# RWKV systems solved in three batches with both directions on 128 partitions, scan offset 4 instead of 8, delta rows padded to 16 bytes

## The chip, the cores and the metric

The kernel runs on one core of a Trainium2 chip. The metric is the device time of one execution in microseconds, as the median of several executions. An execution can be profiled; its profile lists every instruction of the engines PE (TensorE), DVE (VectorE), ACT (ScalarE), POOL (GpSimd) and the DMA issues of SP, ACT and POOL.

## What is computed

Two blocks run one behind the other: a gated convolution with differential attention, and a block whose mixer is half gated delta rule (8 heads of 128) and half RWKV-7 (16 heads of 64), each in both directions over 256 context and 512 latent positions. The change is in the mixers of the second block.

```python
CHUNK = 64
def gated_delta_chunked(q, k, v, beta, g, s0):
    ...
    tmat = lax.linalg.triangular_solve(eye + lmat, eye, left_side=True, lower=True, unit_diagonal=True)
    u = tmat @ (v * beta[..., None])
    wk = tmat @ (kb * jnp.exp(g)[..., None])
    ...
def rwkv7_scan(r, w, k, v, kk, b_vec, s0):
    def step(state, inp):
        sa = -jnp.einsum('bhvk,bhk->bhv', state, kk_t)
        state = (state * w_t[:, :, None, :] + sa[..., None] * b_t[:, :, None, :]
                 + v_t[..., None] * k_t[:, :, None, :])
        return state, jnp.einsum('bhvk,bhk->bhv', state, r_t)
    ...
```

The reference steps RWKV position by position. The kernel does it, like the delta rule, in chunks of 64 positions (12 chunks per direction, the first four of them context, whose outputs aren't needed), and each chunk of each head and direction needs the inverse of a unit triangular 64x64 matrix, called a system here.

## The kernel before

**The systems.** They are formed by the two preparation stages and lie in the tensor `systems`, as 64x64 images, (2 directions) x (96 of the delta rule + 192 of RWKV). `Solver` holds one batch of 96 systems of one direction, one per partition. GpSimd solves it in place (`substitute`): the two 32x32 blocks on the diagonal are inverted in 31 steps of two TENSOR_TENSOR instructions each, L2637 and L2639; `turn` then writes ones on the diagonal (L2645) and two transposed copies (L2652, L2653), from which the scan later builds the off-diagonal block. Direction 2's systems are eliminated backwards (the argument `d`). `begin` fetches a batch (L2665), `end` stores it (L2674), both from GpSimd's own queue. There are six batches: delta, and two of RWKV, for each direction.

**`rwkv_prep`** works through eight pairs of heads, `i`. PE, DVE and ACT form the operands and the systems of pair `i` in direction `d`; SP stores them (`RwkvPrep.store`, L2997 to L3013, the systems at L3000) and counts them in `stored`. Beside that GpSimd solves the batches (0, 0), (0, 1), (1, 0) whole and (1, 1) for `SPLIT` = 20 steps; (1, 0) waits for the stores of the first four pairs.

**`scans`** runs the delta rule's chunks (`DeltaScan`, g) and RWKV's (`RwkvScan`, r) in one loop over n. Loop n holds delta step n and RWKV step n - `LAG`, with `LAG` = 8, so there are 20 loops: eight with a delta step alone, four with both, eight with an RWKV step alone. The order of each engine is written out by hand in one block per engine. GpSimd finishes batch (1, 1), then solves (2, 0) in a room that is later an operand buffer, and (2, 1) in its first room; after that it only zeroes quarters of loaded inverses (`clear`, L3580). SP loads operands two steps ahead: `DeltaOperands.load` has four transfers a step (channel rows L3161 of 129 columns and token rows L3162 of 321), `load_inverse` two (L3167), `RwkvScan.load` eight or twelve, `RwkvScan.load_inverse` four (L3432). In loop `LAG` - 2 SP waits until all stores of GpSimd have landed and loads the first three steps' RWKV inverses. `RwkvScan.middle` (L3444) is the first PE work on an inverse; it stands in the PE's order in loop n for step n + 1 - `LAG`, so everything behind it waits with it. The outputs of the delta steps from 4 on are formed in a bank of their own (`go`) and stored by ACT (`store`). From loop 12 on the PE also folds one head's outputs per loop (`out.fold`), eight in all.

**`closing`** multiplies by the last weights and normalises; it isn't changed.

## Time and profile before

| | us |
|---|---|
| median of 3 runs | 3967.39 (3965.67 to 3968.11) |
| the profiled execution | 3961.41 |
| its span | 3959.7 |
| granted PE clock in it, share of full | 0.932 |
| busy: PE, PEld, DVE, ACT, POOL | 3479.2, 2771.7, 2075.4, 665.0, 787.4 |
| RWKV preparation | 2823 to 3207 |
| scan loops | 3207 to 3694 |
| head outputs, closing | 3694 to 3960 |

All times of the trace are microseconds from the start of the span. PEld is the PE's loading of weights, which overlaps its matmuls. "POOL L2639 TENSOR_TENSOR" is GpSimd's instruction of line 2639. Names such as `all_sn`, `scan_rops` are tiles: `all_sn` is the solver's room, `scan_rops` the RWKV operands (and the second solver's room), `scan_rinv` the RWKV inverses, `all_gchan` and `all_gtok` the delta operands. "SPq" is SP's DMA queue. An instruction's idle time before it stands in brackets with what released it.

### The profile page before, as it was taken

To read this page: it belongs to the slowest core of one execution; us is meant where nothing else is said; L and a number is where in the kernel's file an instruction comes from. 1 tells how busy PE (TensorE), PEld (TensorE's weight loads), DVE (VectorE), ACT (ScalarE), POOL (GpSimd) and SP (SyncE) were. 2 spreads that over 40 slices of the span, in tenths; PEclk is the share of its full clock that TensorE was granted. 3 is DMA by queue.
4 is the path that set the end of the run, shared out by engine and by line. 5 is a ranking of instruction groups with operands and counts; after the bars stand their busy time and mean duration, and the time that the engine had idled before them with its cause. 6 is when DMAs were issued, how large, how long until landed. Compare 5 with 4: busy or idle time off the path is not lost. (4 is left out here: it accounts for less than half of the span.)

```text
span 3959.7 us, 64096 instructions
## 1 busy us (share of the span) xinstructions
PE 3479.2 (88%) x28192; PEld 2771.7 (70%) x28192; DVE 2075.4 (52%) x2261; ACT 665.0 (17%) x1079; POOL 787.4 (20%) x817
## 2 busy tenths in 40 slices
PE   6999999999998989889999999999677725677698
PEld 3777777777787878778888888876466625576386
DVE  2477777753333545544463353329678725332564
ACT  2122222212000001210110010002234301221100
POOL 0111111111000000025005216100375799000000
PEclk8999999999999999999999999999689867888799
DMA  9444444444333453322232223337578798777243
GB/s 400 145 152 147 157 155 149 151 175 161 116 118 111 164 188 138 112 90 88 84 113 86 89 101 107 115 112 258 187 186 225 190 228 169 173 228 213 74 175 106
DMA packets 359079, 607.73 MB, mean 153 GB/s; under 512 B 136441, under 2 KB 244081, under 8 KB 330129
## 3 DMA queue, kind: packets, MB, share of 16 engines
q1 hardware_dynamic: 305488, 472.23, 37.8%
q0 software_dynamic: 21712, 92.42, 7.1%
q10 hardware_dynamic: 31600, 38.99, 2.8%
q8 instruction: 222, 3.64, 0.4%
q14 instruction: 57, 0.46, 0.0%
HBM read 469.17 MB, written 134.39 MB: 152 GB/s over the span
## 5 line engine op out<-in xcount | busy, mean ns | idle before, releaser
L182 PE MATMUL front_ps<-b_hT,p_wb 128*128 128x512 f32 x4224 | 979.3, 392 | 6.8 <-PEq L94 6.8
L182 PEld LDWEIGHTS front_ps<-b_hT,p_wb 128*128 128x128 f32 x4224 | 789.9, 188 | 187.3 <-issue 20.6
L1772 PE MATMUL in_ps<-b_hT,in_wb 128*128 128x512 f32 (+1 forms) x3264 | 750.7, 391 | 13.3 <-DVE in_wb L1759 13.3
L1772 PEld LDWEIGHTS in_ps<-b_hT,in_wb 128*128 128x128 f32 (+1 forms) x3264 | 607.1, 187 | 148.1 <-DVE in_wb L1759 13.5
L1757 DVE CAST in_wb<-in_raw 128x2048 fp32r<-128x2048 f32 (+1 forms) x68 | 82.6, 1215 | 536.4 <-PE in_ps L1772 531.5
L170 DVE CAST p_wb<-p_raw 128x2048 fp32r<-128x2048 f32 x88 | 108.0, 1227 | 430.4 <-PE front_ps L182 419.1
L813 POOL DMA_DIRECT2D front_mwb<-in_w_ada x128 | 101.3, 796 | 794.4 <-PE front_mps L823 788.8
L1772 PEld LDWEIGHTS in_ps<-b_hc,in_wb 128*128 128x128 f32 (+1 forms) x1728 | 211.4, 189 | 3.2
L1772 PE MATMUL in_ps<-b_hc,in_wb 128*128 128x256 f32 (+1 forms) x1728 | 212.6, 283 | 0.0
L172 DVE TENSOR_TENSOR p_wb<-p_raw,p_wb 128x2048 fp32r<-128x2048 f32 x88 | 201.8, 2293 | 3.0
L1211 PE MATMUL mid_ps<-mid_wb,b_hT 128*128 128x512 f32 x768 | 178.2, 393 | 14.0 <-DVE mid_wb L1196 14.0
L1081 PE MATMUL merge_ps<-b_hT,merge_wb 128*128 128x512 f32 x768 | 178.5, 395 | 12.5 <-DVE merge_wb L1069 10.1
L480 DVE SCALAR_TENSOR_TENSOR bf_both<-front_up,front_taps,bf_both 128x512 f32<-128x512 f32 x240 | 180.4, 752 | 11.8
L1211 PE MATMUL last_ps<-last_wb,last_pair 128*128 128x512 f32 x768 | 175.9, 392 | 11.3 <-DVE last_wb L1196 11.3
L1081 PEld LDWEIGHTS merge_ps<-b_hT,merge_wb 128*128 128x128 f32 x768 | 146.1, 191 | 44.9 <-DVE merge_wb L1069 10.5
L1211 PEld LDWEIGHTS mid_ps<-mid_wb,b_hT 128*128 128x128 f32 x768 | 144.5, 189 | 44.1 <-issue 14.4
L1211 PEld LDWEIGHTS last_ps<-last_wb,last_pair 128*128 128x128 f32 x768 | 145.2, 189 | 43.1 <-issue 12.8
L2639 POOL TENSOR_TENSOR all_sn<-all_sn 96x62 f32<-96x62 f32 (+15 forms) x155 | 173.0, 1116 | 12.2
L1759 DVE TENSOR_TENSOR in_wb<-in_raw,in_wb 128x2048 fp32r<-128x2048 f32 (+1 forms) x68 | 173.9, 2557 | 2.3
L2007 POOL TENSOR_TENSOR in_mdx<-in_mx 128x255 f32<-128x255 f32 (+9 forms) x53 | 59.1, 1115 | 526.7 <-ACT in_mx L1984 524.5
L2637 POOL TENSOR_TENSOR all_sn<-all_sn 96x62 f32<-96x62 f32 (+15 forms) x155 | 154.1, 994 | 13.8 <-POOLq L94 1.7
L1790 POOL MEMSET in_gper_row<- 128x2 f32 x1 | 0.1, 99 | 679.4 <-POOLq L94 679.4
(452 smaller groups left out, 4289.0 us busy)
## 6 DMA issues: line engine op xcount, KB each, us to landing
p_raw<-in_w_in_tiles SPq DMA_DIRECT2D x88, 1024.0 KB, 6.1
in_raw<-in_w_in_tiles SPq DMA_DIRECT2D x67, 1024.0 KB, 4.8
front_mwb<-in_w_ada POOLq DMA_DIRECT2D x128, 512.0 KB, 5.0
open_wb<-in_w_ada_groups SPq DMA_DIRECT2D x32, 1024.0 KB, 11.3
g_scr<-gprep_ob SPq DMA_DIRECT2D x8, 3474.0 KB, 11.5
merge_raw<-in_w_branch_units SPq DMA_DIRECT2D x32, 512.0 KB, 4.6
mid_raw<-in_w_o_parts SPq DMA_DIRECT2D x32, 512.0 KB, 3.7
last_raw<-in_w_out_parts SPq DMA_DIRECT2D x32, 512.0 KB, 3.7
```

The source lines that it names most:

```text
L170: nc.vector.tensor_copy(self.wb[:, n % 2, 0], self.raw[:, n % 2]).then_inc(self.high_ok, 1)
L172: nc.vector.tensor_tensor(self.wb[:, n % 2, 1], self.raw[:, n % 2], self.wb[:, n % 2, 0].bitcast(F32), ALU.subtract).then_inc(self.w_split, 1)
L182: last = self.nc.tensor.matmul(self.ps[:, n % 2, :], self.wb[:, n % 2, x, kt, :], self.hT[:, y, kt, :], start=kt == term == 0, stop=kt == ...
L480: link(nc.vector.scalar_tensor_tensor(acc, u[:, j:j + T], self.taps[:, i, j:j + 1], acc, ALU.mult, ALU.add))
L813: pool.dma_start(self.wb[:, m % 2], w[m % 4, :, :, c:c + self.COLS]).then_inc(self.w_in[m % 2], 16)
L1081: last = self.nc.tensor.matmul(self.ps[:, u, :], self.wb[:, u, x, kt, :], self.pair[:, y, j, kt, :], start=kt == n == 0, stop=kt == self.C ...
L1211: last = self.nc.tensor.matmul(self.bank(i), self.pair[:, x, q * self.KQ + kt, t * P:(t + 1) * P], self.wb[:, n % 2, y, kt, :], start=q == ...
L1757: nc.vector.tensor_copy(high, raw).then_inc(self.high_ok, 1)
L1759: nc.vector.tensor_tensor(low, raw, high.bitcast(F32), ALU.subtract).then_inc(self.w_split, 1)
L1772: last = self.nc.tensor.matmul(self.ps[0:width, n % 3, first:end], self.wb[:, n % 2, x, kt, 0:width], h[:, y, kt, :], start=kt == term == ...
L2637: link(ops.tensor_tensor(t, y[:, :, a, j:j + 1].to_broadcast([BATCH, 2, na, ni]), y[:, :, j:j + 1, after].to_broadcast([BATCH, 2, na, ni]) ...
L2639: link(ops.tensor_tensor(y[:, :, a, after], y[:, :, a, after], t, ALU.subtract))
```

## The change

- **Systems.** RWKV's systems get a tensor of their own, `r_systems`, with images of 64 rows by `W` = 96 columns, of which 64 are filled at first and the other 32 later hold the transposed copy. Direction 2's systems are formed transposed (`turned_products`: 48 matmuls of 64 columns in place of 24 of 128 per pair), so that both directions are eliminated forwards, with 64 systems of each direction on 128 partitions: `fetch`, `eliminate`, `deliver`. RWKV then has three batches in place of four, each of 128 systems in place of 96. A batch is fetched in two transfers of 4,096 rows of 256 B (before, one of 96 rows of 16 KB) and stored in two of 64 rows of 24 KB. Batches 0 and 1 need 3 and 6 stored pairs (`ready_by`).
- **Where they run.** In the preparation: delta 0 and 1, RWKV batch 0, and 20 steps of batch 1. In the scan stage: the rest of batch 1, and batch 2, which SP fetches at the stage's start. The second solve in the first room, with its reload by SP, is gone.
- **`LAG`** = 4: 16 loops, four with a delta step alone, eight with both, four with RWKV alone, in which two heads are folded per loop. The inverses are waited for in loop 2.
- **Outputs of the delta steps** are formed in the work banks behind RWKV's `value_outputs`, and ACT stores them ahead of `r.complete`; RWKV has both output banks to itself.
- **Delta rows** are padded: channel rows from 129 to 132 columns (516 to 528 B), token rows from 321 to 324 (1,284 to 1,296 B).
- RWKV inverses are loaded with rows of 384 B in place of 256 B. Addresses move with the sizes, `sw` lies in `ex`, and `r.start` waits for the preparation's stores.

```diff
-G_CH, G_TOK = 2 * C + 1, C + 2 * GD + 1
+G_PAD = 4
+G_CH, G_TOK = 2 * C + G_PAD, C + 2 * GD + G_PAD
...
+W = C + HC
...
+def fetch(eng, m, r_systems, batch):
+    for d in range(2):
+        r = slice(HALF * d, HALF * (d + 1))
+        full = m.image[r].rearrange("p (i j) -> p i j", j=W)
+        eng.dma_start(full[:, :, HC:W], images_of(r_systems, batch, d).rearrange("p (i j) -> p i j", j=W)[:, :, HC:W]).then_inc(m.n_in, 16)
...
+def eliminate(ops, link, m, steps):
+    full, y = m.image.rearrange("p (i j) -> p i j", j=W), m.blocks
+    if steps.start == 0:
+        link(ops.memset(m.diagonal, 2.0))
+    for j in steps:
+        na, ni = j + 1, HC - 1 - j
+        a, after = slice(0, na), slice(na, HC)
+        t = full[:, HC:HC + na, 0:C].rearrange("p a (b y) -> p b a y", b=2)[:, :, :, 0:ni]
+        link(ops.tensor_tensor(t, y[:, :, a, j:j + 1].to_broadcast([P, 2, na, ni]),
+                               y[:, :, j:j + 1, after].to_broadcast([P, 2, na, ni]), ALU.mult))
+        link(ops.tensor_tensor(y[:, :, a, after], y[:, :, a, after], t, ALU.subtract))
...
+def deliver(pool, ops, link, m, r_systems, batch):
...
+    link(ops.memset(m.diagonal, 1.0))
+    flip = lambda x: x.rearrange("p i j -> p j i")
+    link(ops.tensor_copy(full[:, lo, first], flip(full[:, lo, middle])))
+    link(ops.tensor_copy(full[:, hi, first], flip(full[:, lo, last])))
+    link(ops.tensor_copy(full[:, hi, middle], flip(full[:, hi, last])))
+    pool.sem_inc(m.tick, 1)
+    for d in range(2):
+        pool.dma_start(images_of(r_systems, batch, d), m.image[HALF * d:HALF * (d + 1)]).then_inc(m.y_out, 16)
...
-                for n, (batch, d) in enumerate(((0, 0), (0, 1), (1, 0), (1, 1))):
...
+                for d in range(2):
...
+                    solve(nc, pool, link, solver, systems, d, d)
+                for batch in range(BATCHES - 1):
+                    for u in range(3):
+                        pool.wait_ge(m.stored[u], m.STORED * len(range(u, 2 * ready_by(batch), 3)))
+                    pool.wait_ge(solver.y_out, 32 * (batch + 1))
+                    pool.sem_inc(solver.tick, 1)
+                    fetch(pool, solver, r_systems, batch)
...
-LAG = 8
+LAG = 4
+FOLDS = GH // LAG
...
-                sp.dma_start(second.rows, rows_of(systems, 2, 0)).then_inc(second.n_in, 16)
+                fetch(sp, second, r_systems, BATCHES - 1)
                 before.finish_small(sp)
                 r.load(sp, 0)
-                sp.wait_ge(first.y_out, 64)
-                sp.dma_start(first.rows, rows_of(systems, 2, 1)).then_inc(first.again, 16)
...
                     if n == LAG - 2:
-                        sp.wait_ge(second.y_out, 16)
-                        sp.wait_ge(first.y_out, 80)
+                        sp.wait_ge(first.y_out, 32 * BATCHES)
+                        sp.wait_ge(second.y_out, 32)
```

How the instructions move, at two places. Names are tiles and tensors as above, and a row lists the semaphores that it waits for. First GpSimd in the preparation, where one batch is handed over to the next; before, from the first RWKV hand-over (end of the second delta batch, fetch of (1, 0)):

```order
L2652 COPY all_sn<-all_sn 96x32x32 [waits all_schain]
L2653 COPY all_sn<-all_sn 96x32x32 [waits all_schain]
L2674 DMA systems<-all_sn 96x4096 [waits all_schain]
L2665 DMA all_sn<-systems 96x4096 [waits all_sy_out,all_r_stored2,all_r_stored0,all_r_stored1]
L2630 MEMSET all_sn 96x64 [waits all_sn_in]
L2637 TENSOR_TENSOR all_sn<-all_sn 96x62 [waits all_schain]
L2639 TENSOR_TENSOR all_sn<-all_sn 96x2x31 [waits all_schain]
```

Now, at the hand-over from RWKV batch 0 to batch 1:

```order
L2721 MEMSET all_sn 128x64 [waits all_schain]
L2723 COPY all_sn<-all_sn 128x32x32 [waits all_schain]
L2724 COPY all_sn<-all_sn 128x32x32 [waits all_schain]
L2725 COPY all_sn<-all_sn 128x32x32 [waits all_schain]
L2728 DMA r_systems<-all_sn 64x6144 [waits all_schain]
L2728 DMA r_systems<-all_sn 64x6144
L2697 DMA all_sn<-r_systems 64x64x64 [waits all_sy_out,all_r_stored2,all_r_stored0,all_r_stored1]
L2697 DMA all_sn<-r_systems 64x64x64
L2705 MEMSET all_sn 128x64 [waits all_sn_in]
L2711 TENSOR_TENSOR all_sn<-all_sn 128x2x31 [waits all_schain]
```

A third copy stands ahead of the store, store and fetch are two transfers each, and the fetch has rows of 64 elements.

Second SP's queue at the start of the scan stage, behind the operands of RWKV step 0; before:

```order
L3410 DMA scan_rval<-v_scr 128x512
L3412 DMA scan_rval<-v_scr 64x512 [waits open_x_in0]
L3413 DMA scan_rval<-v_scr 64x512
L3823 DMA all_sn<-systems 96x4096 [waits all_sy_out]
L3161 DMA all_gchan<-g_scr 128x8x129 [waits p1_w_in0]
L3162 DMA all_gtok<-g_scr 64x8x321
L3161 DMA all_gchan<-g_scr 128x8x129
L3162 DMA all_gtok<-g_scr 64x8x321
```

Now:

```order
L3484 DMA scan_rval<-v_scr 128x512 [waits open_w_in4]
L3485 DMA scan_rval<-v_scr 128x512
L3487 DMA scan_rval<-v_scr 64x512 [waits open_x_in0]
L3488 DMA scan_rval<-v_scr 64x512
L3242 DMA all_gchan<-g_scr 128x8x132 [waits p1_w_in0]
L3243 DMA all_gtok<-g_scr 64x8x324
L3242 DMA all_gchan<-g_scr 128x8x132
L3243 DMA all_gtok<-g_scr 64x8x324
```

The reload of the first solver's room, with its wait for GpSimd's store, no longer stands ahead of the loads of delta step 2. Further down, the twelve loads of the first RWKV inverses stand ahead of the loads of delta step 5, where before they stood behind those of step 8.

## Rows read from the trace of the kernel before

**Rows 1.** Stretches: length; busy (count) of PE, PEld, DVE, ACT, POOL; clock; DMA share; GB/s.
```profile
2823.00:3207.00 384.00, 260.34 (x3632) 207.38 (x3632) 265.02 (x222) 126.31 (x137) 271.94 (x246) 0.80 0.74 184
3293.00:3348.00 55.00, 41.56 (x725) 36.36 (x723) 33.76 (x44) 11.60 (x24) 50.45 (x53) 0.87 0.92 189
3393.00:3425.00 32.00, 25.63 (x792) 22.91 (x783) 15.19 (x23) 6.94 (x15) 1.21 (x4) 0.89 0.57 110
3425.00:3487.00 62.00, 47.26 (x1375) 42.59 (x1370) 25.60 (x38) 13.93 (x31) 2.43 (x8) 0.81 0.79 197
3487.00:3511.00 24.00, 20.02 (x702) 18.34 (x690) 12.94 (x18) 5.98 (x12) 1.22 (x4) 0.93 0.76 229
3511.00:3694.00 183.00, 131.22 (x4896) 117.46 (x4883) 40.51 (x53) 29.71 (x64) 8.50 (x28) 0.86 0.71 212
```

**Rows 2.** PE waits, 3207 to 3380 us: line and releaser; total, times, longest.
```profile
PE scan_gpx L3444 <- DMA scan_rinv<-systems: 30.8, 1, 30.8
```

**Rows 3.** GpSimd in time, preparation: start, length, instruction, idle before and releaser.
```profile
2832.60 0.21 POOL L2630 MEMSET all_sn<- 96x64 f32 x1 [8.90 <-DMA all_sn<-systems]
...
2909.71 0.21 POOL L2645 MEMSET all_sn<- 96x64 f32 x1 [0.16 <-POOL all_sn L2639]
...
3016.76 0.53 POOL L2674 DMA_DIRECT2D systems<-all_sn  x1 [0.58 <-POOL all_sn L2653]
...
3047.94 0.54 POOL L2665 DMA_DIRECT2D all_sn<-systems  x1 [30.65 <-DMA systems<-rprep_ob]
...
3165.91 0.21 POOL L2630 MEMSET all_sn<- 96x64 f32 x1 [11.95 <-DMA all_sn<-systems]
...
3204.20 1.19 POOL L2639 TENSOR_TENSOR all_sn<-all_sn 96x480 f32<-96x480 f32 x1
```

**Rows 4.** Issues of the RWKV systems' stores, SP: count, ns min/median/max, first and last start.
```profile
L3000 SPq DMA_DIRECT2D systems<-rprep_ob x32: 574/655/1563, 2883.4 to 3194.9; - x32
```

**Rows 5.** GpSimd in time, scan stage.
```profile
3207.06 1.02 POOL L2637 TENSOR_TENSOR all_sn<-all_sn 96x462 f32<-96x462 f32 x1 [1.67 <-POOLq L94]
...
3226.85 0.21 POOL L2645 MEMSET all_sn<- 96x64 f32 x1 [0.15 <-POOL all_sn L2639]
...
3231.58 0.53 POOL L2674 DMA_DIRECT2D systems<-all_sn  x1 [0.59 <-POOL all_sn L2653]
...
3294.66 0.21 POOL L2645 MEMSET scan_rops<- 96x64 f32 x1 [0.15 <-POOL scan_rops L2639]
```

**Rows 6.** SP in time: last stores of the preparation, first inverse loads.
```profile
3201.74 3.64 SPq L3013 DMA_DIRECT2D r_mix<-rprep_ob  x2
...
3374.03 8.47 SPq L3432 DMA_DIRECT2D scan_rinv<-systems  x12
```

**Rows 7.** PE waits, 3393 to 3690 us, the first of the list.
```profile
PE scan_rwork L3462 <- issue: 26.9, 15, 3.9
```

**Rows 8.** Transfers issued from 3207 to 3690 us: count, size, median us to landing.
```profile
all_gtok<-g_scr SPq DMA_DIRECT2D x22, 642.0 KB, 11.9
scan_rops<-r_home SPq DMA_DIRECT2D x24, 528.0 KB, 5.2
...
all_gchan<-g_scr SPq DMA_DIRECT2D x22, 516.0 KB, 9.6
...
systems<-all_sn POOLq DMA_DIRECT2D x2, 1536.0 KB, 8.6
```

**Rows 9.** Transfers, 3376 to 3384 us: packets and the queue's share.
```profile
q1 hardware_dynamic: 5857, 1.47, 82.9%
```

**Rows 10.** GpSimd's transfers of 128 pieces (L2036) and of 512 (L813).
```profile
L2036 POOL DMA_DIRECT2D p<-in_mx x27: 593/602/1584, 1743.6 to 2493.8; - x27
...
DMA to landing us min/median/max: 2.3/2.7/4.3
L813 POOL DMA_DIRECT2D front_mwb<-in_w_ada x128: 748/748/1563, 118.8 to 1010.1; - x128
...
DMA to landing us min/median/max: 4.0/5.0/8.6
```

More of the change, by code:

```diff
@@ L2607, with substitute @@
 BLOCK = HC * C + HC
+W = C + HC
+WIDE = HC * W + HC
 class Solver:
[L2614 removed]
+    AT, SIZE = 78976, 4 * (HC + 2 * WIDE)
     def __init__(self, st, name, room=None):
         if room is None:
[L2618 to L2621 removed]
+            room = st.sb(f"{name}n", [P, HC + 2 * WIDE], at=self.AT)
+        self.n, self.tmp = room[0:BATCH, 0:2 * BLOCK], room[0:BATCH, 2 * BLOCK:2 * BLOCK + HC * HC // 2]
+        self.n_in, self.y_out, self.chain, self.tick = (st.sem(name + x) for x in ("n_in", "y_out", "chain", "tick"))
         self.rows = self.n[:, 0:C * C]
[L2625 removed]
+        self.image = room[:, 0:C * W]
+        self.diagonal = room[:, HC:HC + C * (W + 1):W + 1]
+        self.blocks = room[:, HC:HC + 2 * WIDE].rearrange("p (b r) -> p b r", r=WIDE)[:, :, 0:HC * W].rearrange("p b (i j) -> p b i j", j=W)
+def substitute(ops, link, m, d):
     y = m.n.rearrange("p (b r) -> p b r", r=BLOCK)[:, :, 0:HC * C].rearrange("p b (i j) -> p b i j", j=C)
[L2629 to L2631 removed]
+    link(ops.memset(m.rows[:, 0:C * C:C + 1], 2.0))
+    for step in range(HC - 1):
         j = HC - 1 - step if d else step
@@ L2653, in turn, with rows_of, solve @@
     link(ops.tensor_copy(full[:, near, far], flip(full[:, near, near])))
-def rows_of(systems, batch, d):
-    return systems[d, batch * BATCH:(batch + 1) * BATCH, :]
-SPLIT = 20
-def begin(nc, pool, link, m, systems, batch, d, before):
-    pool.dma_start(m.rows, rows_of(systems, batch, d)).then_inc(m.n_in, 16)
+def rows_of(systems, d):
+    return systems[d]
+def solve(nc, pool, link, m, systems, d, before):
+    pool.dma_start(m.rows, rows_of(systems, d)).then_inc(m.n_in, 16)
     pool.wait_ge(m.n_in, before * 16 + 16)
-    substitute(nc.gpsimd, link, m, d, range(0, SPLIT))
@@ L2670, in end, with images_of @@
-def end(nc, pool, link, m, systems, batch, d):
-    substitute(nc.gpsimd, link, m, d, range(SPLIT, HC - 1))
+    substitute(nc.gpsimd, link, m, d)
     turn(pool, nc.gpsimd, link, m, d)
     pool.sem_inc(m.tick, 1)
-    pool.dma_start(rows_of(systems, batch, d), m.rows).then_inc(m.y_out, 16)
+    pool.dma_start(rows_of(systems, d), m.rows).then_inc(m.y_out, 16)
+HALF = P // 2
+BATCHES = RP * 2 * NCH // HALF
+SPLIT = 20
+def images_of(r_systems, batch, d):
+    return r_systems[d, HALF * batch:HALF * (batch + 1)].rearrange("n s x -> n (s x)")
@@ L3511, in values @@
                 for h in range(2):
-                    last = self.term(self.work[d], q, h, self.inv[:, k % 3, d], self.y[:, d], h, True, True)
+                    last = self.term(self.work[d], q, h, self.inverse(k, d), self.y[:, d], h, True, True)
             last.then_inc(self.s["u_ok"], 1)
@@ L3797, in r_output, with tiles_at, scans @@
         link(nc.vector.tensor_tensor(o, o, self.zr[:, t], ALU.mult))
-LAG = 8
-def scans(nc, k, p2, gain, vectors, bonus, before, given, first, r_scr, v_scr, systems, slots, late, yT):
+LAG = 4
+FOLDS = GH // LAG
+def tiles_at(n):
+    return range(FOLDS * (n - NCH), FOLDS * (n - NCH + 1))
+def scans(nc, k, p2, gain, vectors, bonus, before, given, first, r_scr, v_scr, r_systems, slots, late, yT):
     with Stage(nc, "scan") as st:
@@ L3880, in _ @@
                         r.value_outputs(pe, n - LAG)
+                    if in_g(n) and STEPS[n][2]:
+                        g.outputs(pe, n, 0)
+                        g.outputs(pe, n, 1)
                     if in_g(n):
@@ L3930, in _ @@
                         g.store(act_e, n)
+                    if in_r(n + 1):
+                        r.complete(act_e, n + 1 - LAG)
                     if n >= NCH:
-                        out.take(act_e, n - NCH)
+                        for t in tiles_at(n):
+                            out.take(act_e, t)
                 out.root(act_e)
@@ L3960, in _ @@
                     if n == 0:
-                        r.start(dve)
+                        r.start(dve, before)
                         out.start(dve)
```

203 lines of the change are left out of this document (103 added, 100 removed).

## The prediction, made before the changed kernel was run

> **What bounds the kernel now.** The change touches the stretch from about 2820 us (RWKV preparation) to about 3694 us (last step of the scans). I read first the table of stretches of the scan stage [rows 1], because a share over the whole span would mix stages. It shows three regimes. From 3293 to 3348 us the PE runs delta steps alone: four loops in 55 us, 41.6 us busy, so 13.8 us a loop with 10.4 busy. Then it stands still until 3379 us. From 3393 us loops carry a delta step and an RWKV step (32, 31 and 31 us, the last pair 23.6 busy; the fourth 24 us), and from 3511 to 3694 us RWKV steps alone: eight loops of 22.9 us, 16.4 busy.
>
> The standstill has one cause: the PE waits 30.8 us, to 3379.18 us, for the first RWKV inverses [rows 2]. I followed that wait backwards on GpSimd, in time order. In the preparation it solves systems one behind the other [rows 3, 4]; in the scan stage it finishes one solve and does two more, the first of which ends at 3294.66 us [rows 5]; the inverses are loaded from 3374.03 us [rows 6], behind the store of the last. So the head of the scan is bound by GpSimd, and its tail, 315 us from 3379 to 3694 us (14 of it ahead of the combined loops), by the PE's loops. In the tail the PE's named waits are "issue", 26.9 us in 15 places in front of one line's matmuls alone [rows 7], and no load heads that list, though the DMA share is 0.79 in the combined loops [rows 1].
>
> **Term 1, the preparation: +2 us.** Before, GpSimd does two delta solves, one RWKV solve, and 20 of the 31 steps of the next. After it does the same number, but the RWKV solves have 128 partitions. An operation's elements per partition are the same, so I keep its time: 77.1 us for 31 steps (2832.60 to 2909.71 us [rows 3]), 39.5 us for the last 20 (3165.91 to 3205.4 us). The second delta store is issued at 3016.76 and landed by 3025.4 us (8.6 us [rows 8]). Before, the third solve had to wait for four stored pairs until 3047.94 us; after it needs three. The systems are stored 16 times (two directions of eight pairs), from 2883.4 to 3194.9 us [rows 4], one in 20.8 us; the eighth is issued at 3029 us and its wait ends 19 us later, so the sixth is in by 3006 us and the twelfth, which the next fetch needs, by 3131 us. With F for a fetch: 3025.4 + F + 77.1 + 7.6 (diagonal and three copies; with two copies it is 4.7 us where nothing disturbs it, 3226.85 to 3231.58 us [rows 5]) + 16 (store of 3 MB, at twice those 8.6 us less the part that doesn't grow) + F + 39.5 = 3165.6 + 2F. F is the unknown: two transfers of 4,096 pieces of 256 B, issued by GpSimd, where before one has 96 pieces of 16 KB. From below: pieces of this size move at 5,857 in 8 us at 83% busy [rows 9], so 8,192 take 11.2 us, and with 2.3 us, the least of a transfer on GpSimd's queue [rows 10], 14 us. From above: a transfer of 512 pieces on that queue needs 4.0 us at least and one of 128 pieces 2.3 us [rows 10]; 1.7 us for 384 pieces is 4.4 ns each, 36 us for 8,192, so 38 us. The issuing instruction itself grows by only 0.15 us between the two (602 to 748 ns), 3 us for 8,192. That is nearer to the lower end; I take 21 us. The chain ends at 3207.6 us instead of 3205.4: +2 us (bounds 0, since SP's last store ends at 3205.4 us too [rows 6], and +36). The turned products cost the PE 48 matmuls of 64 columns in place of 24 of 128 in eight places and are covered by the DVE and SP of that stage; without cover they would add some us. The two extra memsets per tile in the delta preparation are 0.5 us at most.
>
> Against the fetch on GpSimd's queue speaks a rule of the Trainium skill ("SBUF — State Buffer", section "SBUF: two separate sides"): a DMA issued from GpSimd has its descriptors made by that engine, and it cannot write them while VectorE holds the port that they share. By it F would be near the upper bound, as the DVE is busy 265 of this stage's 384 us [rows 1]. The trace has long instances that agree, 1,563 to 1,584 ns against medians of 602 and 748 [rows 10].
>
> **Term 2, scan start to the first RWKV middle: −56 us.** Before 3207.06 to 3379.18 us, 172.1 us [rows 5, 2]. After: 11 steps 19.8, deliver 7, one whole solve 63.1 (3231.58 to 3294.66 us), deliver 7, landing of 3 MB 13 (1.5 MB takes 8.6 [rows 8]), the first inverse loads 6 (5.2 before, half as many bytes again): 115.9 us. The third solve of 68 us is gone. The second batch's fetch goes out from SP at the stage's start and has the 27 us of GpSimd's rest of batch 1 to land in. SP no longer waits for a store before it loads delta step 2; that saves nothing, since the PE idles before the first middle anyway.
>
> **Term 3, what the shorter head leaves undone: +62 us.** The lag falls from 8 to 4 because the inverses come earlier, but the PE's idle time was partly filled with delta steps 4 to 7, and they now lie beside RWKV steps. Before: 14 + (32 + 31 + 31 + 24) + 8 × 22.9 = 315 us. After: 8 (rest of loop 3) + four loops like those of before (31 each, 124) + three in which both mixers also form outputs + loop 11 + four with RWKV alone and two folds of the head outputs. For the both-outputs loop: RWKV's share without outputs is 23.6 − 10.4 = 13.2 us busy, with them (and a fold) 16.4, so 26.8 for both, which scaled by 31/23.6 is 35 us. But it also has the loads of the output operands, 1.5 MB: 7.7 MB instead of the 6.1 that fill 31 us at 197 GB/s and a share of 0.79; at the 0.83 of the fullest stretch above [rows 9] that is 37 us. I take 37, three times 111. Loop 11 is 24 + 6 = 30. The last four are 22.9 + 3 = 26, so 104. Sum 377 us: +62. Bounds 345 (combined loops of 28 and 33 us) and 405 (33 and 40). So most of what term 2 gives goes back here: four delta loops of 13.8 us leave cover, and only stalls that overlap are won.
>
> **Term 4, less work for the DMA in the combined loops: −20 us.** Loads of 528 KB in rows of 528 B land in 5.2 us, those of 516 KB in rows of 516 B in 9.6 and those in rows of 1,284 B in 11.9 [rows 8]. Each combined loop has four such delta loads, and the PE's "issue" waits fall where the DMA is full. I take 2.5 us a loop for eight loops, net of inverse rows of 384 B in place of 256 B. Bounds: 0 (the 5.2 us are of loads that go out two at a time, the others four) and −26.
>
> A rule of the skill ("DMA: Bandwidth & Descriptors", section "How a descriptor splits into AXI transactions") says that pieces are moved in beats of 32 B, with a leftover rounded up; rows of 516 B and 528 B then cost the same 17 beats when aligned, and the padding gives nothing. The measured 9.6 against 5.2 us leans the other way, but does not separate alignment from queueing.
>
> **Sum**: +2 − 56 + 62 − 20 = −12, and half a us for the memsets: 3961.4 − 11.5 = 3950 us for an execution like the profiled one, which ran 6.0 us under the median of 3967.4. Against that median: 3956 us.
>
> **Rivals.**
> (a) *The fetches bind the preparation (slower).* Two fetches of 35 to 38 us put its end at 3165.6 + 74 = 3240 us: +34 in place of +2, so about +20 us, 3988 us. It decides from F = 27 us on, where the sum is zero. For it: rows of 256 B from GpSimd occur nowhere in the trace. Against: the issue instruction's small growth. Chance 0.13.
> (b) *Combined loops are longer and padding gives nothing (slower).* With 33 and 39 us a loop, term 3 is 8 + 132 + 117 + 33 + 104 = 394, +79, and term 4 about −8: sum +17, 3984 us. For it: the DMA is at 0.8 in loops that don't yet load RWKV's output operands, and those four loads join the delta loads in loops 8 to 11. Against: PE rows name no load. Chance 0.17.
> (c) *Padding gives half* (−10): sum −1, 3966 us, within 0.2%. By the skill's rule on beats alone term 4 is 0 and the sum +8, 3975 us. Together 0.20.
> (d) *The overlap is better*, 29 and 34 us: term 3 is 8 + 116 + 102 + 30 + 104 = 360, +45: sum −29, 3939 us. Chance 0.13.
> (e) The forecast, −5 to −20 us: 0.37.
>
> 0.2% is 8 us, about what a measurement of this kernel can tell from no change. Faster: (e) and (d), 0.50. Same: (c), 0.20. Slower: (a) and (b), 0.30. The range leaves out the far ends of (a), (b) and (d): 3930 to 3992 us.
>
> **What would show it.** GpSimd: the first fetch's 128-partition memset some 21 us behind its issue; the stage's end within 5 us of 3207 (over 3225 is rival a). The first RWKV middle near 3325 us. Loops 4 to 7 at 28 to 29 us with padding, 8 to 10 at 34 to 35; the end of the last step 8 to 15 us before 3694. DVE waits or named loads in loops 8 to 11 would make term 3 wrong; gchan still landing in over 9 us, term 4.

## The result, and the profile after

| | before | changed |
|---|---|---|
| median, us | 3967.7 (3965.7 to 3968.1, 4 runs) | 4002.2 (3997.7 to 4007.8, 4 runs) |
| ratio | | 1.0097 (95% interval 1.0082 to 1.0112) |
| the profiled execution; its span | 3961.4; 3959.7 | 4007.8; 4006.1 |
| DMA: packets, MB | 359079, 607.73 | 367977, 614.95 |

The change makes the kernel 1.0% slower; forecast were 3956 us and, at most, 3992. The profiled execution of the changed kernel is the slowest of its four, 5.6 us over their median.

Four marks divide the difference. In the list of one line's instructions "a to b" are the first and the last start, and the marks are read from there in every run below: the first matmul of the scan stage (the end of the preparation), the first RWKV middle, and the last fold.

| us | before | changed | difference |
|---|---|---|---|
| end of the preparation | 3207.1 | 3225.2 | +18.1 |
| from there to the first RWKV middle | 172.1 | 118.7 | −53.4 |
| from there to the last fold (the tail) | 313.9 | 391.2 | +77.3 |
| from there to the end of the span | 266.6 | 271.0 | +4.4 |

The marks of the changed kernel, PE instructions of the middle and of the fold (last start 3735.1), where before has 3379.2 and 3693.1:

```profile
L3520 PE MATMUL scan_gpx<-scan_rinv x768: 184/212/258, 3343.9 to 3692.7; 32*32 32x32 f32 x192
...
L3763 PE MATMUL scan_gwork<-scan_o_fold,b2y_y2T x64: 216/421/473, 3649.7 to 3735.1; 128*128 128x64 f32 x64
```

GpSimd of the changed kernel in order of time; it answers to [rows 3] and [rows 5]:

```profile
3023.23 3.30 POOL L2697 DMA_DIRECT2D all_sn<-r_systems  x2 [9.00 <-DMA r_systems<-rprep_ob]
3039.55 0.22 POOL L2705 MEMSET all_sn<- 128x64 f32 x1 [13.03 <-DMA all_sn<-r_systems]
...
3112.38 0.22 POOL L2721 MEMSET all_sn<- 128x64 f32 x1 [0.15 <-POOL all_sn L2713]
...
3120.54 1.13 POOL L2728 DMA_DIRECT2D r_systems<-all_sn  x2 [0.61 <-POOL all_sn L2725]
...
3154.81 3.28 POOL L2697 DMA_DIRECT2D all_sn<-r_systems  x2 [33.13 <-DMA r_systems<-rprep_ob]
3171.48 0.21 POOL L2705 MEMSET all_sn<- 128x64 f32 x1 [13.39 <-DMA all_sn<-r_systems]
...
3225.16 1.02 POOL L2711 TENSOR_TENSOR all_sn<-all_sn 128x462 f32<-128x462 f32 x1 [12.99 <-POOLq L93]
...
3314.28 0.21 POOL L2721 MEMSET scan_rops<- 128x64 f32 x1 [0.15 <-POOL scan_rops L2713]
...
3320.99 1.09 POOL L2728 DMA_DIRECT2D r_systems<-scan_rops  x2 [0.58 <-POOL scan_rops L2725]
```

A fetch with its wait takes 16.3 us (3023.23 to 3039.55) and 16.7 us; its issue 3.3 us for two. The sequence in the scan stage is as forecast: 89 us from the start to the end of the elimination, store, first middle at 3343.9. What isn't is the start itself. GpSimd waits 13.0 us ahead of it, so it doesn't set it, and 33.1 us before its second fetch, for stored systems that the forecast had landed by 3131 us (the fetch goes out at 3154.81). SP's queue ends last:

```profile
3120.12 1.33 SPq L3074 DMA_DIRECT2D r_systems<-rprep_ob  x2
...
3122.85 18.30 SPq L3079 DMA_DIRECT2D r_read<-rprep_ob  x1
...
3220.39 3.50 SPq L3086 DMA_DIRECT2D r_mix<-rprep_ob  x2
...
3337.51 2.61 SPq L3507 DMA_DIRECT2D scan_rinv<-r_systems  x4
```

Its last store ends at 3223.9 us (3205.4 before [rows 6]). At 3122.85 us one issue of a 256 KB store takes 18.3 us. The transfers of the 16 us from 3120 us, by queue (packets, MB, share) and by kind (median to landing last), show what is under way beside it: GpSimd's 3 MB store has 85% of the DMA engines' time and SP's queue 7%, and two of SP's stores land in 23 to 24 us.

```profile
q0 software_dynamic: 134, 2.90, 84.7%
q1 hardware_dynamic: 882, 0.22, 7.0%
...
r_home<-rprep_ob SPq DMA_DIRECT2D x1, 792.0 KB, 23.2
...
r_read<-rprep_ob SPq DMA_DIRECT2D x1, 256.0 KB, 24.4
```

SP's late stores come back to the engine that fills them. VectorE (DVE) has three buffers `rprep_ob` for the operands of a pair, and waits until one is stored. Its waits for that in the preparation (total, times, longest) and the stretch of the whole preparation (columns as in [rows 1]):

```profile
DVE rprep_ob L2862 <- DMA r_mix<-rprep_ob: 19.6, 2, 11.8
```

```profile
2823.00:3225.00 402.00, 264.89 (x4016) 212.98 (x4014) 264.76 (x218) 124.69 (x136) 274.77 (x249) 0.81 0.74 181
```

The list of the kernel before has no such wait. VectorE is busy as long as before (264.8 us, 265.0 in [rows 1]) and waits 19.6 us more, where the stage is 18.1 us longer. One wait, of 7.8 us, ends at 3044.5 us behind GpSimd's first fetch, the other, of 11.8 us, at 3176.5 us behind its store and second fetch.

The PE's waits from 3200 to 3420 us (line and releaser; total, times, longest). The wait for the inverses is still there [rows 2], and one of 24 us for the rows of delta step 2:

```profile
PE scan_gpx L3520 <- DMA scan_rinv<-r_systems: 38.1, 1, 38.1
PE scan_gwork L3319 <- DMA all_gtok<-g_scr: 24.1, 1, 24.1
```

And the stretches behind the first middle (columns as in [rows 1]): four loops without RWKV outputs, three with both, loop 11, and the last four.

```profile
3360.00:3497.00 137.00, 98.08 (x2799) 87.66 (x2796) 51.79 (x77) 28.30 (x61) 3.64 (x12) 0.82 0.78 184
3497.00:3611.00 114.00, 82.69 (x2550) 75.59 (x2543) 42.50 (x63) 20.85 (x45) 3.65 (x12) 0.84 0.86 211
3611.00:3639.00 28.00, 22.36 (x786) 20.09 (x782) 13.62 (x19) 5.46 (x11) 1.22 (x4) 0.95 0.67 179
3639.00:3737.00 98.00, 78.22 (x2378) 70.20 (x2376) 20.73 (x27) 16.35 (x34) 2.43 (x8) 0.80 0.65 193
```

The loops without outputs take 34.2 us (137 for four) and those with both 38.0, at 24.5 and 27.6 us busy: the busy time is within 1 us of the forecast (23.6, 26.8), and the loops are 3.2 and 1.0 us longer than its 31 and 37 us.

### The profile page after: what moved, and what is told of

The parts are those of the page before. It is cut to its first block and busy times, and to the rows that moved or that the text cites. A ratio compares the mean times of both kernels' runs of the same rounds, so it can differ in the third digit from the quotient of the medians.

```text
span 4006.1 us, 64829 instructions
## 1 busy us (share of the span) xinstructions
PE 3506.3 (88%) x28576; PEld 2791.8 (70%) x28576; DVE 2070.6 (52%) x2265; ACT 665.4 (17%) x1079; POOL 733.4 (18%) x758
## 2 busy tenths in 40 slices
DMA packets 367977, 614.95 MB, mean 154 GB/s; under 512 B 144696, under 2 KB 252336, under 8 KB 339408
## 5 line engine op out<-in xcount | busy, mean ns | idle before, releaser
L479 DVE SCALAR_TENSOR_TENSOR bf_both<-front_up,front_taps,bf_both 128x512 f32<-128x512 f32 x240 | 180.4, 752 | 11.8
L1210 PEld LDWEIGHTS last_ps<-last_wb,last_pair 128*128 128x128 f32 x768 | 145.1, 189 | 43.1 <-issue 12.9
L2976 PE MATMUL rprep_ps_m<-rprep_ob,rprep_kT 64*64 64x128 f32 x768 | 59.8, 322 | 49.5 <-issue 49.5
L2976 PEld LDWEIGHTS rprep_ps_m<-rprep_ob,rprep_kT 64*64 64x64 f32 x768 | 55.7, 166 | 56.6 <-issue 56.6
```

The costliest lines, as they stand in the source:

```text
L479: link(nc.vector.scalar_tensor_tensor(acc, u[:, j:j + T], self.taps[:, i, j:j + 1], acc, ALU.mult, ALU.add))
L1210: last = self.nc.tensor.matmul(self.bank(i), self.pair[:, x, q * self.KQ + kt, t * P:(t + 1) * P], self.wb[:, n % 2, y, kt, :], start=q == ...
L2976: last = self.nc.tensor.matmul(ps[r, c * width:(c + 1) * width], lhs[r, c * C:(c + 1) * C], rhs(r, c), start=True, stop=True)
```

## Experiments

Times of several executions are compared as ratios with the kernel before on the same chip. Runs without an interval have one execution and are read by their marks alone. Six kernels that keep the old loop (before, f3, h2, h3, i3, j1) have a tail of 307 to 314 us, which is the spread to keep in mind.

### f1: the changed kernel with offset 8

```diff
-LAG = 4
+LAG = 8
...
-    return range(FOLDS * (n - NCH), FOLDS * (n - NCH + 1))
+    return range(GH * (n - NCH) // LAG, GH * (n - NCH + 1) // LAG)
```

> The changed kernel with a scan offset of 8 in place of 4 (one head folded per loop again); everything else is kept. Theory A (the offset itself is the loss: delta steps 4 to 7 fill the PE's wait for the inverses and cost nothing there, but 34 us a loop beside RWKV steps): the PE reaches loop 7 about 56 us behind the end of loop 3 (3305 us), so the first RWKV middle comes at about 3361 us instead of 3344, the tail behind it takes 315 to 320 us as in the kernel before in place of 393, and the time falls by 55 to 65 us against the changed kernel, to about 3943 us: under both kernels. Rival B (the tail is longer because RWKV's steps themselves are slower: wider inverse rows, outputs moved into the work banks): the tail stays over 350 us and the time within 20 us of the changed kernel's 4002.

Ratio 1.0048 (1.0031 to 1.0065): half of the loss is gone, not all. The marks:

```profile
L3294 PE MATMUL scan_gpx<-all_ginv x384: 191/191/258, 3219.0 to 3470.0; 32*32 32x32 f32 x192
...
L3520 PE MATMUL scan_gpx<-scan_rinv x768: 184/191/258, 3384.4 to 3679.7; 32*32 32x32 f32 x192
...
L3763 PE MATMUL scan_gwork<-scan_o_fold,b2y_y2T x64: 216/323/474, 3544.6 to 3710.4; 128*128 128x64 f32 x64
```

The tail is 326.0 us, 65.2 shorter than with offset 4: not quite the 315 to 320 of theory A, and far from the 350 of rival B. But the first middle is at 3384.4, not 3361, and the time falls by 0.5%, some 20 us, and not by 55 to 65. The PE reaches loop 7 late, since it waits for token rows at steps 2, 4, 5 and 7 (24.8, 3.6, 8.2 and 3.7 us), and then waits 13.5 us more for the inverses. Theory A holds for the tail and fails for the head; 12 us of the tail's growth stay at offset 8.

### f2 and f3: the padding alone

```diff
-G_PAD = 4
+G_PAD = 1
```

and, for f3, in the kernel before:

```diff
-G_CH, G_TOK = 2 * C + 1, C + 2 * GD + 1
+G_PAD = 4
+G_CH, G_TOK = 2 * C + G_PAD, C + 2 * GD + G_PAD
```

> The changed kernel with delta rows of 129 and 321 columns again (no padding). If the padding relieves the loads as term 4 had it, this is 15 to 25 us slower than the changed kernel (about 4020 us). If rows of 516 and 528 B cost the same and the landing times are queueing, it is within 5 us of 4002, and the channel loads still land in about 9 us.

> The kernel before with nothing but the padded delta rows (132 and 324 columns). If padding gives 2.5 us per combined loop, there are four such loops here and four loops of delta steps: 10 to 20 us faster than before. If it gives nothing: within 5 us of before.

f2: 1.0107 (1.0073 to 1.0140), beside 1.0097 (1.0082 to 1.0112) with padding; its tail is 389.4 us (3338.0 to 3727.4), against 391.2. f3: 1.0002 (0.9986 to 1.0019). The padding gives nothing that these intervals could show in either kernel; the 20 us of term 4 are 0.5%. In the changed kernel the channel rows land in 8.9 us (9.6 before), without padding (f2) in 9.5, and padded in the old kernel (f3) in 9.7. The rows of RWKV's step operands, which always had 528 B, now land in 8.9 us too (5.2 before [rows 8]):

```profile
all_gtok<-g_scr SPq DMA_DIRECT2D x22, 648.0 KB, 11.1
scan_rops<-r_home SPq DMA_DIRECT2D x24, 528.0 KB, 8.9
all_gchan<-g_scr SPq DMA_DIRECT2D x22, 528.0 KB, 8.9
...
scan_rinv<-r_systems SPq DMA_DIRECT2D x48, 192.0 KB, 4.9
```

With offset 8, in f1, the same operand rows are back at 5.7 us:

```profile
scan_rops<-r_home SPq DMA_DIRECT2D x24, 528.0 KB, 5.7
```

So the 5.2 against 9.6 us on which term 4 rested came of where the loads stand among others, not of the length of a row.

### f4, g1, g2, h1, h2: what lengthens the preparation

f4 takes GpSimd's RWKV solves out of the preparation and does them in the scan stage:

```diff
-                for batch in range(BATCHES - 1):
...
-                    fetch(pool, solver, r_systems, batch)
...
-                        eliminate(nc.gpsimd, link, solver, range(0, SPLIT))
...
-                eliminate(nc.gpsimd, first.link, first, range(SPLIT, HC - 1))
-                deliver(pool, nc.gpsimd, first.link, first, r_systems, BATCHES - 2)
+                for batch in range(BATCHES - 1):
...
+                    fetch(pool, first, r_systems, batch)
+                    pool.wait_ge(first.n_in, 32 * (batch + 2))
+                    eliminate(nc.gpsimd, first.link, first, range(0, HC - 1))
+                    deliver(pool, nc.gpsimd, first.link, first, r_systems, batch)
```

> The changed kernel with GpSimd solving only the two delta batches in the preparation; all three RWKV batches are solved in the scan stage, so the PE waits some 250 us longer there and the whole time is some 170 us longer; what is read is the end of the preparation. Theory C (GpSimd's fetches of 4,096 small rows and its 3 MB stores hold up SP's stores, which set the end of the stage): the preparation ends at 3190 to 3207 us. Rival D (the turned products, the strided stores of the systems or the shared buffer of sw are slower): it still ends at 3220 us or later.

g1 puts the transfers back into the preparation, without the solving (a memset of the room, 5.2 us, stands ahead of them, and the store right behind the first fetch, at 3048.7 us in place of 3120.5):

```diff
+                for batch in range(BATCHES - 1):
...
+                    fetch(pool, solver, r_systems, batch)
+                    pool.wait_ge(solver.n_in, 32 * (batch + 2))
+                    if batch < BATCHES - 2:
+                        for d in range(2):
+                            pool.dma_start(images_of(r_systems, batch, d), solver.image[HALF * d:HALF * (d + 1)]).then_inc(solver.y_out, 16)
```

> The kernel of f4 (all RWKV solves in the scan stage), with the transfers of the changed kernel put back into the preparation, without the elimination: GpSimd fetches batch 0 when three pairs are stored and stores the images again unchanged (3 MB), and fetches batch 1 when six pairs are stored. f4's preparation ended near 3178 us, the changed kernel's at 3219 to 3225. If the transfers hold up SP's stores (theory C), most of these 41 to 47 us come back: an end past 3200 us. If GpSimd's arithmetic slows the DVE (rival E), the end stays within 8 us of f4's.

g2 puts the arithmetic back, without transfers:

```diff
+                    if batch == 0:
+                        link(nc.gpsimd.memset(solver.image, 0.0))
+                        eliminate(nc.gpsimd, link, solver, range(0, HC - 1))
...
+                    else:
+                        eliminate(nc.gpsimd, link, solver, range(0, SPLIT))
```

> The same kernel f4 with the other half put back: GpSimd runs the elimination of 31 and then 20 steps and the three copies in the preparation, on a room filled with zeros, with no transfer. Its result isn't used; the real solves are in the scan stage. Theory C: the preparation ends within 8 us of f4's 3178 us. Rival E: past 3200 us, with DVE instructions that take longer.

h1 is g1 without the store, and h2 is f4's edit made in the kernel before:

> The kernel of f4 (all RWKV solves in the scan stage; its preparation ends at 3178 us) with only the two fetches of 4,096 + 4,096 rows of 256 B put back into the preparation, without the 3 MB store that g1 also had (g1 ended at 3205 us). If the small rows are what holds up SP, the preparation ends at 3195 us or later. If it is the bytes (2 + 3 + 2 MB in g1), the two fetches are 4 of 7 MB and it ends near 3193; if it is the store with its rows of 24 KB, it ends under 3185.

> The kernel before, with its two RWKV solves of the preparation moved to the scan stage as in f4. If the turned products, the strided stores and the shared buffer of the change cost the preparation nothing, it ends at 3175 to 3181 us as f4's did, and the kernel before pays 27 us for GpSimd's part there, the changed one 41 to 47. If it ends under 3170, those parts cost the difference.

The first matmul of the scan stage of each, in the order f4, g1, g2, h1, h2:

```profile
L3281 PE MATMUL scan_gpx<-all_ginv x384: 191/191/258, 3177.6 to 3685.2; 32*32 32x32 f32 x192
```

```profile
L3293 PE MATMUL scan_gpx<-all_ginv x384: 191/191/258, 3205.3 to 3711.9; 32*32 32x32 f32 x192
```

```profile
L3294 PE MATMUL scan_gpx<-all_ginv x384: 191/191/258, 3205.2 to 3707.6; 32*32 32x32 f32 x192
```

```profile
L3288 PE MATMUL scan_gpx<-all_ginv x384: 191/191/258, 3192.4 to 3699.0; 32*32 32x32 f32 x192
```

```profile
L3213 PE MATMUL scan_gpx<-all_ginv x384: 191/191/258, 3182.1 to 3566.2; 32*32 32x32 f32 x192
```

- f4 3177.6 and h2 3182.1: with no RWKV solve beside it the changed preparation is not longer than the old one. Turned products, strided stores and the shared buffer cost nothing that shows (rival D falls).
- h1 3192.4: the two fetches give +14.8 us. g1 3205.3: with the store +27.7, so the store of 3 MB is 12.9 of it. By h1's own terms that is the reading by bytes (4 of 7 MB, an end near 3193), not by the number of small rows.
- g2 3205.2: the arithmetic alone gives +27.6. C and E were put as alternatives, and each alone lengthens the stage by the same 28 us.
- Together 55 us; the changed kernel has 40 to 49 over f4 (3217.7 to 3226.7 in the five profiles that have its preparation), the kernel before 25 over h2 (3207.1).

How the arithmetic does it is seen in one VectorE instruction behind 3017 us, first in f4, where GpSimd does nothing there, then in g2, where it eliminates (count | busy us, mean ns | idle us before):

```profile
L2862 DVE TENSOR_TENSOR rprep_bT<-rprep_kk,rprep_rate 128x768 f32<-128x768 f32 x8 | 7.7, 958 | 0.3
```

```profile
L2862 DVE TENSOR_TENSOR rprep_bT<-rprep_kk,rprep_rate 128x768 f32<-128x768 f32 x8 | 12.5, 1562 | 0.3
```

958 ns become 1,562. With the transfers alone (g1) it stays at 958. The transfers act by the other way, VectorE's wait for a stored buffer: 16.1 us in g1, 8.3 in h1, none in f4 and g2.

Which of the two ways sets the changed kernel apart from the kernel before is seen in two sums for VectorE, from 2823 us to each kernel's own end of the preparation:

| us | end | VectorE busy | its wait for a stored `rprep_ob` |
|---|---|---|---|
| h2, before without RWKV solves | 3182.1 | 248.5 | 0 |
| before | 3207.1 | 265.0 | 0 |
| f4, changed without RWKV solves | 3177.6 | 242.5 | 0 |
| changed | 3225.2 | 264.8 | 19.6 |
| its four variants f1, f2, g3, g4 | 3217.7 to 3226.7 | 266.0 to 267.3 | 18.1 to 19.6 |

The arithmetic costs about the same in both kernels: 16.5 us of busy time over h2 in the one and 22.3 over f4 in the other, to the same 265 us; g2 alone has 282.9, more than the changed kernel pays. What is new is the wait, so the +18 us come by the transfers (2 + 3 + 2 MB for RWKV where before there were three of 1.5) and not by the arithmetic. Nor does GpSimd now work where it had idled: before, it waited 30.7 us for the fourth pair [rows 3], now 9.0 and 33.1 us for the third and the sixth.

### g3 and g4: offset 6, and SP's order at offset 8

g3 is f1's edit with `LAG = 6`. g4 is f1 with SP's loads in another order:

```diff
-                r.load(sp, 0)
                 for n in range(NCH + LAG):
...
-                    if n == LAG - 2:
+                    if n == 2:
+                        r.load(sp, 0)
+                    if n == LAG - 3:
```

> The changed kernel with a scan offset of 6. Measured: offset 4 has its first RWKV middle at 3344 us and a tail of 393 us, offset 8 at 3384 and 327. If a delta step beside an RWKV step costs 16 to 17 us more than none, the tail is 360 us here. The middle is then set by the inverses or by the PE's loop 5, at 3345 to 3355 us: an end of the scans near 3708 us and a time 2 to 6 us under f1's.

> The kernel of f1 (offset 8) with SP's queue reordered: the operands of RWKV step 0 are loaded behind those of delta step 4 instead of at the stage's start, and the first inverses behind those of delta step 7 instead of step 8. In f1 the PE waited 25 us for the token rows of delta step 2, and the inverses were issued only at 3373 us, though their stores had landed by about 3335. Expected: the wait at step 2 falls under 10 us, the first middle comes at 3355 to 3362 us in place of 3384, the tail keeps its 327 us: 20 to 28 us under f1, which is within 8 us of the kernel before. If the DMA is simply full in this stretch, the PE's waits only move to later delta steps and the gain is under 8 us.

g3: 1.0059 (1.0043 to 1.0075), first middle and last fold:

```profile
L3294 PE MATMUL scan_gpx<-all_ginv x384: 191/191/258, 3217.7 to 3505.7; 32*32 32x32 f32 x192
...
L3520 PE MATMUL scan_gpx<-scan_rinv x768: 185/194/258, 3351.6 to 3676.0; 32*32 32x32 f32 x192
...
L3763 PE MATMUL scan_gwork<-scan_o_fold,b2y_y2T x64: 275/275/473, 3585.5 to 3711.8; 128*128 128x64 f32 x64
```

The tail is 360.2 us, where 360 was expected: the three offsets lie nearly on a line, 326.0, 360.2, 391.2, or 16.3 us for each delta step that stands beside an RWKV step instead of in front. But the time isn't under f1's, since what the head gains (133.9 us in place of 165.4) the tail loses. g4: 1.0049 (1.0033 to 1.0066), no gain. The wait at delta step 2 fell (24.8 to 11.7 us), the one at step 5 rose (8.2 to 11.7 us), and all waits for token rows together went from 40.8 to 31.9 us. The head is 14 us shorter than f1's, but the tail of this execution is 350.7 us (3378.2 to 3728.9) in place of 326.0, and no run shows why. As this execution was 17 us over the median of its kernel, the marks say little of the other four; that the gain is missing is all that g4 shows.

### i1 and i2: the moved outputs, and the offset in the old layout

i1 moves the delta outputs in the kernel before; i2 adds `LAG = 4`:

```diff
-                            g.state_outputs(pe, n, 0)
...
                         r.value_outputs(pe, n - LAG)
+                    if in_g(n) and STEPS[n][2]:
+                        g.outputs(pe, n, 0)
+                        g.outputs(pe, n, 1)
```

> The kernel before with only the delta outputs moved as in the change (formed in the work banks behind RWKV's value outputs, stored by ACT ahead of RWKV's completion, the state update waiting for the store). If this makes the tail behind the first middle longer, it is 324 to 330 us in place of 316 (f1 had 327). If the wider inverse rows do it, it stays at 312 to 319 us.

> The same kernel with a scan offset of 4 and two heads folded per loop: the kernel before in its systems, its loads and its rows, with the changed loop. If the offset costs what it does between f1 and the changed kernel, the tail is 66 us longer than i1's, the first middle stays at about 3379 us, since the solves set it, and the time is 60 to 70 us over the kernel before. If the offset is cheap with narrow inverse rows and few bytes, the tail grows by under 40 us.

i1:

```profile
L3436 PE MATMUL scan_gpx<-scan_rinv x768: 184/191/258, 3385.1 to 3674.8; 32*32 32x32 f32 x192
...
L3675 PE MATMUL scan_gwork<-scan_o_fold,b2y_y2T x64: 216/275/473, 3543.7 to 3707.2; 128*128 128x64 f32 x64
```

i2:

```profile
L3436 PE MATMUL scan_gpx<-scan_rinv x768: 185/191/258, 3377.0 to 3730.2; 32*32 32x32 f32 x192
...
L3675 PE MATMUL scan_gwork<-scan_o_fold,b2y_y2T x64: 275/275/473, 3686.4 to 3767.4; 128*128 128x64 f32 x64
```

i1's tail is 322.1 us, 8 over before and outside the spread of 307 to 314, in one execution (its time, 18 us over before, also holds a preparation that ended 5.6 us later). It lies between the two expectations: the outputs' new place seems to account for 8 of the 12 us that f1 kept, and the other 4 are within the spread. i2's is 390.4: the offset costs 68.3 us in the old layout (65.2 in the new one), and its time is 83 us over before. So the offset makes most of the longer tail by itself, with the old systems, loads and rows.

### h3, i3, j1: an earlier start of GpSimd in the kernel before

h3 loosens one wait, for batch (1, 0), and does 28 steps of the next batch in the preparation; i3 also moves SP's loads of RWKV step 0 behind delta step 4's and its reload of the first room behind delta step 2's; j1 also puts the second solver's fetch first:

```diff
-SPLIT = 20
+SPLIT = 28
...
                     if batch == 1 and d == 0:
...
+                        for u in range(3):
+                            pool.wait_ge(m.stored[u], m.STORED * len(range(u, RP - 1, 3)))
+                    if batch == 1 and d == 1:
                         for u in range(3):
                             pool.wait_ge(m.stored[u], m.STORED * len(range(u, RP, 3)))
...
-                g.load(sp, 1)
                 before.finish(sp)
                 sp.dma_start(second.rows, rows_of(systems, 2, 0)).then_inc(second.n_in, 16)
+                g.load(sp, 1)
```

> The kernel before with one wait loosened: batch (1, 0), direction 1 of the first four pairs, is fetched when the seventh store has landed in place of the eighth (its systems are all in the first seven), and 28 in place of 20 steps of batch (1, 1) are done in the preparation. Theory F (the head of the scan is bound by GpSimd's chain of solves alone; the PE idles 31 us there): GpSimd starts that batch some 11 to 18 us earlier, the last store of the scan stage goes out as much earlier than 3366 us, the first RWKV middle comes at 3361 to 3368 us in place of 3379, the tail of 315 us behind it moves with it: 10 to 17 us faster than before. Rival G (the preparation's SP queue and the DMA give it back, as in the changed kernel): the preparation ends later by what is won, and the time is within 4 us of before.

h3: 0.9990 (0.9976 to 1.0003). The fetch of (1, 0) went out 14.6 us earlier (3033.3 us) and the preparation ended 2.4 us later, so rival G is not what happened; nor did the first middle come earlier (3379.7 us), as theory F had it. GpSimd's store in the scan stage went out at 3217.29 instead of 3231.58, and then GpSimd stood:

```profile
3217.29 0.53 POOL L2674 DMA_DIRECT2D systems<-all_sn  x1 [0.59 <-POOL all_sn L2653]
3232.59 0.21 POOL L2630 MEMSET scan_rops<- 96x64 f32 x1 [14.77 <-DMA scan_rops<-systems]
```

The wait that took the place of the one removed is the second solver's fetch from SP's queue.

> The kernel of h3 (batch (1, 0) one store earlier, 28 steps of (1, 1) in the preparation) with SP's loads of RWKV step 0 moved behind those of delta step 4, so that the second solver's fetch has fewer transfers beside it. In h3 that fetch was issued at 3212.6 and ended GpSimd's wait at 3232.6 us, 15 us after its store. If the loads beside it made it long, the wait ends at 3226 to 3228 us, the first middle comes 4 to 7 us earlier than 3379, and the time is 5 to 10 us under before. If the last stores of the preparation are what it waits behind, nothing moves and the time is within 4 us of before.

i3: 0.9997 (0.9985 to 1.0009). The fetch was issued at 3209.5, SP issued nothing more until 3223.2, and GpSimd's wait ended 20 us behind the issue again: here the loads behind it made no difference.

```profile
3229.64 0.21 POOL L2630 MEMSET scan_rops<- 96x64 f32 x1 [14.97 <-DMA scan_rops<-systems]
```

> The kernel of i3 with the second solver's fetch ahead of the four loads of delta step 1 on SP's queue. If these loads are what the fetch stood behind, GpSimd's wait for it (to 3229.6 us, 20 us after the issue) ends 8 to 12 us earlier, the first RWKV middle comes at 3365 to 3370 us in place of 3376 to 3380, and the time is 6 to 12 us under the kernel before; delta step 1 is 8 to 12 us later, which the PE's 35 us of idle time hides. If the fetch stands behind the last stores of the preparation, the wait ends within 3 us of before and the time is the same.

```profile
3214.83 0.53 POOL L2674 DMA_DIRECT2D systems<-all_sn  x1 [0.58 <-POOL all_sn L2653]
3217.00 0.21 POOL L2630 MEMSET scan_rops<- 96x64 f32 x1 [1.64 <-DMA scan_rops<-systems]
...
3353.04 0.53 POOL L3997 DMA_DIRECT2D systems<-all_sn  x1 [0.57 <-POOL all_sn L2653]
```

j1: 0.9967 (0.9951 to 0.9983), 13 us under the kernel before and 1.3% under the changed one. The fetch lands by 3217.0 us, 10 us after its issue, GpSimd's last store goes out at 3353.04 instead of 3366.62, and the first middle is at 3368.2. As this is the only edit against i3, what held the fetch was the four transfers ahead of it on its own queue. They now come later, and the PE's waits for token rows are 40.4 us in six places (34.1 in four before), which still leaves it 18.6 us of waiting for the inverses. The first middle of j1, in the list of its line:

```profile
L3447 PE MATMUL scan_gpx<-scan_rinv x768: 184/191/258, 3368.2 to 3644.1; 32*32 32x32 f32 x192
```

## Why the prediction was wrong

- **Term 1, +2 us: failed.** Measured +18, and +11 to +20 in all five profiles of this preparation. F was well chosen (21 for 16.3 us). The step that failed is the bound "0, since SP's last store ends at 3205.4 us too": it took the end of SP, and of VectorE ahead of it, as fixed, and put at nothing what GpSimd's transfers do to SP's stores. They held these up until VectorE waited 19.6 us for a free buffer, where before it waited for none. Against f4, with no RWKV solve beside the stage, the fetches give +15, the 3 MB store +13 and the arithmetic +28 one by one, but the arithmetic was paid before as well. GpSimd's own chain ran late with it: the second fetch went out at 3154.8 us, when the sixth pair's stores had landed, where the sum has 3147.
- **Term 2, −56 us: held.** −53.4.
- **Term 3, +62 us: held for the offset**, 65 to 68 us by f1 and i2. It left out the moved outputs, 8 us in i1's one execution. By the stretches the tail is 393 us where the forecast had 377. The difference lies in the rest of loop 3 (16 in place of 8 us), the four loops without outputs (137 in place of 124) and the three with both (114 in place of 111); loop 11 and the last four were 8 us shorter than forecast.
- **Term 4, −20 us: failed.** Nothing in f2 and f3. It is the term that made the forecast a gain: without it the sum is +8. The working itself named the reason (two loads against four in the queue) and then took 20 of a range from 0 to 26. The sign named for it, channel rows landing in over 9 us, would have missed it: they land in 8.9 us (9.5 in f2), and the kernel takes as long. The rule of the Trainium skill on beats ("DMA: Bandwidth & Descriptors", section "How a descriptor splits into AXI transactions"), by which aligned rows of 516 and 528 B need the same number, agrees with both runs.
- **The sum.** +18 − 53 + 77 + 4 = +46 in the profiled execution; forecast −12. Of the miss of 58 us terms 4 and 1 are 36, what stays of the tail at offset 8 is 12, and the rest is the offset (3), term 2 (3) and the stretch behind the last fold (4).
- **The rivals.** (a) had the right place, the end of the preparation, and the wrong mechanism: it wanted slow fetches on GpSimd's chain, and they were fast. The Trainium skill's rule that VectorE keeps GpSimd from writing descriptors ("SBUF — State Buffer", section "SBUF: two separate sides") was read as putting F near 38 us; the trace has 16.3. The section says it of VectorE operations in a two-port mode, and the costliest of this stage's are TENSOR_TENSOR and scans. (b) had both its halves, loops of 34 and 38 us and no gain from padding, but with term 1 at +2 it stopped at 3984.
- **The range.** (a) and (b) were never added to each other, though nothing on record kept both from coming true. (a) is 32 us over the forecast and (b) 28; both together would have been 4016 us, and the measured 4002 lies between.
- **What the kernel would have told.** The PE's idle time in front of the first middle was the cover of four delta steps. The change shortens the wait by 53 us and at once takes 65 us of work out of its cover.

Left open: how much of f1's 12 us are the wider inverse rows; what makes the combined loops 1 to 3 us longer than forecast; why GpSimd's large transfers hold up SP's stores as they do; and why the part behind the last fold is 4 us longer (i1, which moves only the outputs, has 270.6 us there, where the six kernels with the old loop have 266 to 270).

## What to carry to other kernels

Idle time of an engine may be holding up other work's cost: ask what runs inside a wait before paying for a shorter one, and price the work that leaves it at its cost beside the rest, not at its busy time. Landing times of two loads in different places of a queue say nothing of their shapes. A bound read from another engine's end holds only while what stands beside that engine stays the same: here more bytes on GpSimd's queue delayed the stores on SP's, and VectorE, two steps away, waited for its buffers.

## What the runs showed of the hardware

- GpSimd's queue has far fewer packets than rows. In the 18 us of the first fetch it moved 2.10 MB of 256-byte rows in 544 packets, 3.9 KB each on the average, where SP's queue has one packet a row (in 8 us 5,857 packets for 1.47 MB [rows 9]):

```profile
q0 software_dynamic: 544, 2.10, 52.6%
...
all_sn<-r_systems POOLq DMA_DIRECT2D x2, 1024.0 KB, 13.0
```

- Beside GpSimd's 3 MB store in rows of 24 KB, SP's small ones hardly move: 84.7% against 7.0% of the engines' time in the 16 us above, with one issue of SP held for 18.3 us and two stores landing in 23 to 24 us.
- A VectorE TENSOR_TENSOR on two SBUF inputs of 128x768 takes 958 ns with GpSimd idle or only transferring (f4, g1) and 1,562 ns on the average beside its elimination (g2), and the whole stage is 28 us longer by it. One with an input in PSUM (`rprep_ps_m`, 128x1536) takes 1,758 ns in all three.
- A transfer's time depended on what its own queue held ahead of it, not behind: 20, 20 and 10 us for the same 1.5 MB in h3, i3 and j1.
- In the RWKV-only loops of the kernel before, 3511 to 3691 us, the PE's waits called "issue" that are over 0.6 us long come once every 127 to 140 matmuls or at a multiple of that, 26 of them. So they follow the count of instructions; no run shows their cause.
